# The combine stage of a decoder step: normalisation moved between engines, gathers four tiles deep

## The reference

```
y = _moe(h, router_w, router_b, e_w_gate[l], e_w_up[l], e_w_down[l])
x = _layer_norm(ALPHA * x + gate2 * y, ln_g[l, 1], ln_b[l, 1])
```

## Time and profile before

| What | Value |
|---|---|
| median of three runs | 2730.56 us |
| the profiled execution, its own time | 2736.39 us |
| its span in the trace | 2734.8 us |
| last stage, from its first DMA issue to the end of the span | 2640.20 to 2734.8 us |
| busy over the whole span | TensorE 86%, VectorE 51%, ScalarE 38%, GpSimd 13% |
| busy in 2640 to 2735 | TensorE 0, VectorE 62.5 us, ScalarE 24.1 us, GpSimd 49.9 us |

### The profile page before, as it was taken

One profiled execution on the slowest core, in us unless ns is written; L12 is line 12 of the kernel. 1 busy time (PEld: TensorE's weight loads), 2 busy tenths in 40 slices (PEclk: granted clock), 3 DMA queues, 4 the chain that ended last, 5 costly groups with the idle time before them and its releaser, 6 DMA issues. The chain is left out here.

```text
span 2734.8 us, 40039 instructions
## 1 busy us (share of the span) xinstructions
PE 2346.0 (86%) x11749; PEld 1767.7 (65%) x11749; DVE 1393.9 (51%) x2311; ACT 1034.4 (38%) x1735; POOL 342.9 (13%) x403
## 2 busy tenths in 40 slices
PE   2999998887949999999598999999989499999940
PEld 0876665666838788787387565555668377788730
DVE  2412311457866655664581343333368666655738
ACT  1211220543125655653441443433331265654623
POOL 0000000550000100100110323000000010101115
PEclk9899999788959999999897999999999599999975
DMA  6156654845037867874654544222250388866944
GB/s 258 47 185 211 222 188 134 210 128 194 39 121 269 305 230 252 300 261 151 212 180 140 178 130 139 89 88 89 93 194 39 120 277 293 291 228 224 341 138 149
DMA packets 193833, 501.71 MB, mean 183 GB/s; under 512 B 19362, under 2 KB 39299, under 8 KB 187236
## 3 DMA queue, kind: packets, MB, share of 16 engines
q1 hardware_dynamic: 165140, 405.11, 44.2%
q0 software_dynamic: 19056, 66.20, 7.0%
q10 hardware_dynamic: 9536, 29.13, 2.8%
HBM read 434.76 MB, written 68.77 MB: 184 GB/s over the span
## 5 line engine op out<-in xcount | busy, mean ns | idle before, releaser
L1817 DVE TENSOR_TENSOR e_wl<-e_raw,e_wh 128x1024 fp32r<-128x1024 f32 x384 | 449.2, 1219 | 97.9 <-ACT e_wh L1728 97.7
L1728 ACT CAST e_wh<-e_raw 128x1024 fp32r<-128x1024 f32 x384 | 382.1, 1048 | 96.5 <-DMA e_raw<-in_e_up 39.3
L1647 PE MATMUL e_psG<-e_wh,e_xh 128*128 128x512 f32 x784 | 321.6, 410 | 10.2 <-issue 7.4
L1649 PE MATMUL e_psG<-e_wh,e_xl 128*128 128x512 f32 x784 | 311.8, 398 | 0.0
L1648 PE MATMUL e_psG<-e_wl,e_xh 128*128 128x512 f32 x784 | 310.6, 396 | 0.0
L1647 PE MATMUL e_psY<-e_wh,e_hh 128*128 128x512 f32 x392 | 159.8, 408 | 23.1 <-DVE e_hl L1840 23.1
L519 PE MATMUL in_ps<-in_w_upper,in_h_upper 128*128 128x512 f32 (+1 forms) x432 | 178.6, 413 | 0.0
L1647 PEld LDWEIGHTS e_psG<-e_wh,e_xh 128*128 128x128 f32 x784 | 148.9, 190 | 42.8 <-issue 8.3
L520 PE MATMUL in_ps<-in_w_lower,in_h_upper 128*128 128x512 f32 (+1 forms) x432 | 172.7, 400 | 0.0
L1649 PEld LDWEIGHTS e_psG<-e_wh,e_xl 128*128 128x128 f32 x784 | 148.4, 189 | 37.0
L521 PE MATMUL in_ps<-in_w_upper,in_h_lower 128*128 128x512 f32 (+1 forms) x432 | 171.9, 398 | 0.0
(11 more groups left out here) (527 smaller groups left out, 4450.9 us busy)
## 6 DMA issues: line engine op xcount, KB each, us to landing
e_raw<-in_e_gate SPq DMA_DIRECT2D x32, 2048.0 KB
e_raw<-in_e_up SPq DMA_DIRECT2D x32, 2048.0 KB, 8.4
e_raw<-in_e_down SPq DMA_DIRECT2D x32, 2048.0 KB, 7.8
x<-in_ada_w SPq DMA_DIRECT2D x40, 1024.0 KB, 5.4
yrows<-e_y ACTq DMA_DIRECT2D x49, 512.0 KB, 8.1
x<-in_cache SPq DMA_DIRECT2D x64, 320.0 KB, 3.4
a_pages<-in_cache SPq DMA_DIRECT2D x64, 320.0 KB, 3.5
in_w_raw<-in_a_w_in POOLq DMA_DIRECT2D x48, 256.0 KB, 4.6
```

The source lines that it names most:

```text
L1647: T.matmul(out, upper[:, k, :], wh[:, z, cols], start=k == 0, stop=False)
L1649: mm = T.matmul(out, lower[:, k, :], wh[:, z, cols], start=False, stop=k == PIECES * n - 1)
L1728: S.copy(wh[:, z, c * PC:(c + 1) * PC], raw[:, z, c * PC:(c + 1) * PC]).then_inc(s_hi[z], 1)
L1817: V.tensor_tensor(wl[:, z, at], raw[:, z, at], wh[:, z, at].bitcast(F32), ALU.subtract).then_inc(s_lo[z], 1)
```

## The change

The stage is written anew with the same arithmetic in another order:

- Gathers: `ya` and `yb` have four buffers. GpSimd only gathers: tiles 0 to 3 at once, tile t after `both(t - 4)`.
- The gate multiplication is on VectorE (`gated`).
- Statistics: VectorE's residual instruction also writes its row sum (`total`, `accum_out`), a small instruction makes -mean of it; ScalarE squares (z - mean) with a row sum (`accum_out`), and takes the root of sum/1024 + eps. `bn_stats` and `bn_aggr` are gone.
- VectorE makes (z - mean) * g in one instruction (`centred`) straight into `g.x`.
- TensorE, for the prompt's tiles: ones (33 x 128, float32r) times two rows with b, then diag(1/deviation) (128 x 128, float32) times `g.x`, added up in PSUM, in halves of 512 columns. ScalarE makes the diagonal from `g.ident`, and copies the result from PSUM to `g.x` (`out`), one tile late.
- The sample tile ends on VectorE with one instruction, times 1/deviation plus b.
- SyncE loads the prompt's gate first, g after the first gather has landed, the sample's gate and b after `centred(0)`. Its store loop is unrolled.

```diff
+            load_mods(sp, g, gate[:, 0, :], layer, GATE2, False, s_gate)
+            sp.wait_ge(s_zero, 1)
+            sp.dma_start(lb33[0:1, :], g.ln_b[r:r + 1, :]).then_inc(s_lb, 16)
+            sp.dma_start(lb33[32:33, :], g.ln_b[r:r + 1, :]).then_inc(s_lb, 16)
+            sp.wait_ge(s_g[0], 32)
+            sp.dma_start(lg[:], g.ln_g[r:r + 1, :].broadcast_to([P, D])).then_inc(s_lg, 16)
+            sp.wait_ge(s_cen, 1)
+            load_mods(sp, g, gate[:, 1, :], layer, GATE2, True, s_gateS)
+            sp.dma_start(lbS[:], g.ln_b[r:r + 1, :].broadcast_to([NSAMP, D])).then_inc(s_lbS, 16)
...
+            for t in range(RING):
+                gather(t)
+            for t in range(RING, TILES):
+                po.wait_ge(s_both, t - RING + 1)
+                gather(t)
...
+            pe.wait_ge(s_low, 1)
+            for t in range(PT):
+                par = t % 2
+                pe.wait_ge(s_diag, t + 1)
+                pe.wait_ge(s_cen, t + 1)
+                if t >= 2:
+                    pe.wait_ge(s_x, t - 1)
+                for a in range(2):
+                    cols = slice(a * HALF, (a + 1) * HALF)
+                    T.matmul(psN[:, par, cols], ones[:], both_rows[:, cols], start=True, stop=False)
+                    T.matmul(psN[:, par, cols], diag[:, par, :], g.x[:, t, cols], start=False, stop=True).then_inc(s_mm, 1)
...
+            def first(t):
+                n, r = rows_of(t), t % RING
+                act.wait_ge(s_g[r], 32 * (t // RING) + 32)
+                if t >= RING:
+                    act.wait_ge(s_cen, t - RING + 1)
+                S.activation(zr[0:n, r, :], ya[0:n, r, :], ACT.Copy, scale=g.weight[0:n, 0, t:t + 1]).then_inc(s_first, 1)
+            def out(t):
+                for a in range(2):
+                    act.wait_ge(s_mm, 2 * t + a + 1)
+                    S.copy(g.x[:, t, cols], psN[:, t % 2, cols])
+                act.drain()
+                act.sem_inc(s_x, 1)
...
+            for t in range(3):
+                first(t)
             for t in range(TILES):
+                act.wait_ge(s_mean, t + 1)
+                S.activation(junk[0:n, :], zr[0:n, t % RING, :], ACT.Square, bias=nmean[0:n, par:par + 1],
+                             accum_out=ssq[0:n, par:par + 1])
+                act.drain()
+                act.sem_inc(s_ss, 1)
+                act.wait_ge(s_ss, t + 1)
+                S.activation(sd[0:n, par:par + 1], ssq[0:n, par:par + 1], ACT.Sqrt, bias=eps[0:n, :], scale=1.0 / D
+                             ).then_inc(s_dev, 1)
+                if t + 3 < TILES:
+                    first(t + 3)
+                if t < PT:
+                    act.wait_ge(s_rec, t + 1)
+                    S.activation(diag[:, par, :], g.ident[:], ACT.Copy, scale=sd[:, par:par + 1]).then_inc(s_diag, 1)
+                if t >= 1:
+                    out(t - 1)
...
+            def residual(t):
+                v.drain()
+                V.scalar_tensor_tensor(out=z, in0=g.x[0:n, t, :], scalar=ALPHA, in1=z, op0=ALU.mult, op1=ALU.add,
+                                       accum_out=total[0:n, par:par + 1])
+                v.drain()
+                V.tensor_scalar(nmean[0:n, par:par + 1], total[0:n, par:par + 1], -1.0 / D, None, ALU.mult)
+                v.drain()
+                v.sem_inc(s_mean, 1)
+            def centred(t):
+                V.scalar_tensor_tensor(out=g.x[0:n, t, :], in0=zr[0:n, t % RING, :], scalar=nmean[0:n, par:par + 1],
+                                       in1=lg[0:n, :], op0=ALU.add, op1=ALU.mult).then_inc(s_cen, 1)
+            def reciprocal(t):
+                v.wait_ge(s_dev, t + 1)
+                V.reciprocal(d, d).then_inc(s_rec, 1)
...
             both(0)
+            gated(0)
+            both(1)
             for t in range(TILES):
+                residual(t)
                 if t + 1 < TILES:
+                    gated(t + 1)
+                if t == 0:
+                    v.wait_ge(s_lg, 16)
+                centred(t)
+                reciprocal(t)
+                if t + 2 < TILES:
+                    both(t + 2)
+            v.wait_ge(s_lbS, 16)
+            v.drain()
+            V.scalar_tensor_tensor(out=g.x[0:n, PT, :], in0=g.x[0:n, PT, :], scalar=sd[0:n, par:par + 1], in1=lbS[:],
+                                   op0=ALU.mult, op1=ALU.add)
+            v.drain()
+            v.wait_ge(s_x, PT)
+            v.sem_inc(s_x, 1)
```

More of the change, by code:

```diff
@@ L2036, in stage_combine @@
         RING = 4
[L2037 to L2044, removed]
+        zr, junk = sb("z", [P, RING, D]), sb("squares", [P, D])
+        total, nmean, ssq, sd = (sb(n, [P, 2]) for n in ("total", "minus_mean", "sum_squares", "sd"))
+        eps, diag = sb("eps", [P, 1]), sb("diagonal", [P, 2, P])
+        lg, lbS, gate = sb("lg", [P, D]), sb("lb_sample", [NSAMP, D]), sb("gate", [P, 2, D])
+        lb33, both_rows, ones = sb("lb33", [33, D]), sb("lb_rows", [33, D], F32R), sb("ones33", [33, P], F32R)
+        ya, yb = sb("ya", [P, RING, D]), sb("yb", [P, RING, D])
+        psN = ctx.enter_context(nc.psum_tensor(f"c{layer}_psN", [P, 2, D], F32))
+        s_zero, s_lb, s_lg, s_lbS, s_gate, s_gateS, s_row, s_low = (sem(x) for x in (
+            "rows_zeroed", "lb_loaded", "lg_loaded", "lb_sample_loaded", "gate_loaded", "gate_sample_loaded",
+            "lb_upper", "lb_lower"))
+        s_first, s_both, s_mean, s_ss, s_dev, s_cen, s_rec, s_diag, s_mm, s_x, s_st = (sem(x) for x in (
+            "first_weighted", "both_summed", "mean_ready", "squares_summed", "deviation", "centred", "reciprocal",
+            "diagonal_ready", "scaled", "x_ready", "y_stored"))
+        s_g = [sem(f"rows_gathered{r}") for r in range(RING)]
         block = ctx.enter_context(nc.Block())
@@ L2072, in _ @@
[L2072 to L2081, removed]
+                                                 ).then_inc(s_g[r], 16)
+            for t in range(RING):
+                gather(t)
@@ L2095, in _ @@
+            S.activation(junk[:, 0:1], g.ones[:, 0:1], ACT.Sqrt)
+            S.copy(ones[:], g.ones[0:33, :])
+            act.wait_ge(s_lb, 32)
+            S.copy(both_rows[:], lb33[:]).then_inc(s_row, 1)
+            for t in range(3):
+                first(t)
             for t in range(TILES):
                 n, par = rows_of(t), t % 2
[L2097 to L2100, removed]
@@ L2108, in _ @@
             V = nc.vector
[L2109 removed]
+            V.memset(lb33[:], 0.0)
+            V.memset(eps[:], EPS)
+            v.drain()
+            v.sem_inc(s_zero, 1)
             def both(t):
[L2112 to L2115 removed]
@@ L2117, in finish @@
[L2117 to L2120, removed]
-                v.drain()
-                V.tensor_tensor(g.x[0:n, t, :], z, lb[0:n, :], ALU.add).then_inc(s_x, 1)
+                n, r = rows_of(t), t % RING
+                z = zr[0:n, r, :]
+                v.wait_ge(s_first, t + 1)
+                V.scalar_tensor_tensor(out=z, in0=yb[0:n, r, :], scalar=g.weight[0:n, 1, t:t + 1], in1=z,
+                                       op0=ALU.mult, op1=ALU.add).then_inc(s_both, 1)
@@ L2130, in _ @@
[L2130 to L2138, removed]
```

55 lines of the change are left out of this document (24 added, 31 removed).

## The result

The changed kernel takes 2702.01 us (median of four runs, 2697.67 to 2703.76) beside 2728.76 us before (2725.1 to 2738.34). The ratio is 0.9894, with a 95% interval of 0.9866 to 0.9923: 26.8 us (1.1%) faster by the medians, 21 to 37 by the interval. I had predicted 2705 us, 25.8 us faster. The profiled execution took 2701.83 us, its span is

What follows compares the result with a forecast made beforehand. VectorE was taken to bound the middle of the last stage, late first rows and gate values its head. Gains 10.4 + 11.7 + 3.7 = 25.8 us from the median 2730.56 gave 2704.8, predicted 2705; forecast's range 2699 to 2713, eight in ten 2698 to 2716.

Steps and rivals of the forecast that it cites:

- the head: Stage start up to both(2): first pair lands earlier, both(2) at 2658.9 in place of 2669.31, 10.4 us gained.
- the middle: both(2) to both(8): six tiles at 5.5 us, 33.0 instead of 44.7, 11.7 us gained.
- the end: both(8) to the end of the span: 17.1 us instead of 20.8, 3.7 gained, with TensorE on the path.
- VectorE's tile: VectorE's steps per tile sum to 5.33 us, plus 0.19 for the accumulator's read; 5.5 taken.
- The rule against the accumulator: Residual on VectorE: with two SBUF sources not bf16, no read port is left for the accumulator, so half throughput.
- The third rival: VectorE's residual: the accumulator costs a second pass, 1.0 us more on each of nine tiles, 2714 us; chance 0.06.
- The transfers: Gathers and stores: 4.8 us a tile, hidden under 5.5; the rival that they bound the middle, 2713 us, had chance 0.17.
- TensorE: Its matmuls take 4.3 us a tile, hidden but for the last tile; 6.3 if weight loads are not covered.
- ScalarE: Its work per tile sums to 4.6 us, hidden under 5.5, not waiting for TensorE's result except for tile 7.
- the second rival: TensorE or ScalarE bounds the tile at 6.3 us, shown by ScalarE waiting for `psN`: 2711 us; chance 0.07.
- The round trip: Mean through ScalarE, VectorE and TensorE to the copy and next mean, 11.9 us; forecast to overlap between tiles.
- the slower rival: One tile's chain from mean to copy must end before the next mean: 2743 us, slower than before; chance 0.04.

Runs made afterwards that it cites:

- bn_stats: Changed kernel with bn_stats and bn_aggr back on VectorE and no square on ScalarE: 42.36 us for six tiles (7.06 each), 61.2 from both(2) to the end.
- scale_on_vector: Changed kernel with TensorE's part undone, VectorE scaling by 1/deviation and adding b for all tiles: 40.81 us for six tiles, 58.1 from both(2) to the end.
- before_four_deep: Kernel before with four buffers for gathered rows and gathers four tiles ahead: both(2) 22.5 us after first issue, six tiles 45.8, stage 89.2.
- no_ones: Changed kernel without TensorE's 16 matmuls of ones with b: six tiles 32.97 us, end 14.85, stage 66.3.
- te_order: Changed kernel with both matmuls of ones ahead of the waits for diagonal and g.x, then both diagonal matmuls: stage 65.6 us, end 15.5.
- two_deep: Changed kernel with two buffers for gathered rows in place of four: 41.75 us for six tiles, 61.2 from both(2) to the end.
- combined: Changed kernel with gate and g spread from rows by TensorE, ones matmuls ahead of the waits, last prompt tile scaled on VectorE: stage 65.7 us, whole kernel 2702.93.
- gate_on_gpsimd: Changed kernel with the gate multiplication back on GpSimd: 34.15 us for six tiles, stage 71.5.

## Why the prediction was right

The time, the sum and the mechanism of the head and of the middle were right. Part of the closeness is luck. The stage gained 26.2 against 25.8 because two misses cancelled: the head gained 1.1 more than forecast, the end 0.7 less. The head of the kernel before differs by 1.8 between its two profiles, so 11.5 there could as well have been 9.7.

- **VectorE's tile**: 5.33 + 0.19 predicted, 5.43 measured. The accumulator's read costs next to nothing: the residual takes 1.31 to its successor, and 1.30 in `bn_stats`, where it has no accumulator. The other 0.1 is spread over the steps, half of it in the centred pass (1.20, I had 1.15). The contention with GpSimd went, and every pass takes 1.22 to 1.28. `bn_stats` and `scale_on_vector`, which add terms back, came out within 0.03 and 0.1 us a tile of their sums. That six tiles are 32.95 and not 32.6 comes from one of them, which takes 5.82 (2671.10 to 2676.92), with 0.58 of "issue" before the gated pass; it is there in each variant that has this order of instructions on VectorE, and not in `bn_stats` and `scale_on_vector`, whose tile has others. I have no cause for it. The kernel before has the like: the prediction took its 0.17 a tile, 1.05 us over the six, for waits for gathers, but 0.40 of them go with such a gap, 0.47 of "issue" before one addition of b (2697.29). Only the other 0.65, in the next tile, come from a late root, ahead of which ScalarE had waited for rows.
- **The rule against the accumulator**, which the prediction cites from the Trainium skill, does not hold here: the residual with `accum_out` and two float32 sources in SBUF takes 1.23 us, beside 1.216 without. The third rival falls.
- **The head**: 10.4 predicted, 11.5 measured. The second `both` came 11.7 us after the first issue, 1.4 sooner than in my schedule; the bytes moved faster there than the 350 GB/s that I took from the row (376 to 409). The third pair came when I had it, at 14.8. The prediction gives the gain as one sum, and when I split it, for `before_four_deep`, I gave the depth 0 to 2 us where it has 5 to 7.
- **The transfers** are hidden in the middle: no wait for rows in four-deep rings. With two buffers they are not.
- **TensorE** is the step that was mis-sized: 4.3 predicted, 5.45 measured, and the first diagonal it never caught up with. I took each matmul from a stretch where its like followed it (the earlier trace rows has another float32 matmul next, another float32r one); here the two kinds alternate, and each half paid 0.3 twice. My bound of 6.3 had it inside. It cost nothing in the middle, where it lies 0.03 over VectorE's 5.42 and the lag stayed within the double buffer. At the end the last store is issued 10.3 us after the last prompt mean, where the forecast's terms give 9.1. Of these 1.2 us the end shows 0.7 (17.85 against 17.1), because the mean came 0.25 earlier and the store took 0.4 less than I had them. That it cost so little was luck: TensorE had no room left, and with a quicker VectorE it would have bounded the whole middle.
- **ScalarE**: busy 22.56 of 33 us in the window after, no wait of VectorE on it in the middle, as forecast. Against the forecast it waits for TensorE in every tile, 0.2 to 0.6 us each in the middle. The sign of the second rival was there, its cost was not.
- **The round trip** overlaps, and the slower rival did not arise.

## What to carry to other kernels

Price a moved instruction by its neighbours in the new order, not by the row where it follows its like: on TensorE a change between two kinds of weights cost what made a hidden engine a bound. When a stage ends the program, reorder its last tile so that the path with the fewest hand-overs comes last; either of two such edits gave 2.3 to 2.6 us at the end, both together no more. And compare the stage from its own first issue: the stages before it moved by 20 us from run to run, the stage of the kernel before by one.

## What the runs showed of the hardware

TensorE, busy in all of 33.00 us, stayed at the lower level of the clock (0.50). In `no_ones` the granted clock was higher in three windows (the third, from 2690, at 0.88), and in `te_order` in two (the other at 0.67):

```profile
2660.00:2670.00 10.00, 5.71 (x8) 1.85 (x8) 9.28 (x15) 6.96 (x14) 5.63 (x4) 0.78 1.00 330
2670.00:2680.00 10.00, 6.25 (x8) 2.00 (x8) 8.89 (x13) 7.06 (x13) 0.76 (x1) 0.73 0.40 151
```

```profile
2660.00:2670.00 10.00, 6.95 (x13) 2.30 (x12) 9.28 (x13) 6.96 (x14) 6.39 (x4) 0.82 1.00 339
```

Idle time as such is not what these have in common. `two_deep` and `bn_stats` leave TensorE idle too (busy 29.3 and 32.3 of the 40 us from 2654) and stood at 0.50 throughout. In `no_ones`, `te_order` and `combined` (0.75 from 2654 to 2688) the two diagonal matmuls of a tile follow each other; in the kernels that stayed at 0.50 a matmul of ones stands between them. No run isolates this, and I know no cause.

VectorE's pass with two inputs in SBUF stood still until GpSimd's multiplication ended (2.93 us in place of 1.28), which is what the Trainium skill says of the port that they share (SBUF — State Buffer, "Who interferes with whom": the later one is blocked for the whole instruction). The trace agrees, and the small loss of the pass with g in the earlier trace rows (1.50 us) is the same thing met late. GpSimd's multiplication beside it was

```profile
2685.21 3.26 POOL L2079 TENSOR_TENSOR c_z<-c_z,c_gate 128x1024 f32<-128x1024 f32 x1 [0.83 <-DVE c_z L2114]
```

It ended at 2688.47, and the pass, begun 0.42 before that, ended 1.08 after it: in `gate_on_gpsimd` this was 1.09. What such a pass loses is the time for which GpSimd still had to run when it began (1.84 and 0.42), less 0.1 to 0.2. The reverse shows too: this multiplication began beside the residual, which started first (2685.05) and kept its 1.22, and took 3.26 us, where the one at 2656.20, with VectorE idle as it began, took 2.34.
